# Two hybrid blocks on one Trainium2 core: dilated attention with bias and maximum in one instruction, queries scaled on GpSimd, block turns later, and spreads by transposes

## The reference

```python
def rms_norm_2(x, w):
    xf = x.astype(jnp.float32)
    y = xf * lax.rsqrt(jnp.mean(xf * xf, axis=-1, keepdims=True) + EPS)
    return (y * w.astype(jnp.float32)).astype(x.dtype)

# in second_block, for each layer:
q = rms_norm_2(q.reshape(b, s, ATT_HEADS, ATT_HEAD_DIM), q_norm[i])
k = rms_norm_2(k.reshape(b, s, ATT_HEADS, ATT_HEAD_DIM), k_norm[i])
y_att = dilated_attention(q, k, v).reshape(b, s, ATT_WIDTH)
x = x + jnp.concatenate([y_ssd, y_att], axis=-1) @ w_out[i]

# dilated_attention: for each of the branches ((128, 1), (512, 4), (2048, 16))
scores = jnp.einsum("bnqrhe,bnkrhe->bnrhqk", qb, kk).astype(jnp.float32)
scores = scores * (1.0 / math.sqrt(e))
scores = jnp.where(valid, scores, -jnp.inf)     # causal, one key in `dilation`
p = jnp.exp(scores - jnp.max(scores)); o = (p / den) @ v
# the three branches are then weighed by the softmax of their log denominators
```

## Time and profile before

| what | us |
|---|---|
| median of three runs | 1941.1 (1940.7 to 1943.38) |
| the profiled execution, its time | 1941.14 |
| its span, first to last instruction | 1939.3 |
| TensorE busy | 1912.3 (99%) |
| DVE, ACT, GpSimd busy | 1440.1, 1156.5, 375.9 |

### The profile page before, as it was taken

One profiled execution on the slowest core, in us unless ns is written; L12 is line 12 of the kernel. 1 busy time (PEld: TensorE's weight loads), 2 busy tenths in 40 slices (PEclk: granted clock), 3 DMA queues, 4 the chain that ended last, 5 costly groups with the idle time before them and its releaser, 6 DMA issues.

```text
span 1939.3 us, 30473 instructions
## 1 busy us (share of the span) xinstructions
PE 1912.3 (99%) x11704; PEld 1666.5 (86%) x11704; DVE 1440.1 (74%) x2535; ACT 1156.5 (60%) x2112; POOL 375.9 (19%) x424
## 2 busy tenths in 40 slices
PE   9999999999999999999999999999999999999999
PEld 8878998887899988888887788888888897878887
DVE  5866976576688759765687878866885678887874
ACT  6666765565676545554666655555554566656552
POOL 1110222011012104420012204411440002122430
PEclk9999999999999999999999999999999999999999
DMA  8434556543445555555553346555555544345654
GB/s 299 139 104 146 186 185 234 178 135 124 139 160 190 198 186 181 188 189 171 183 172 103 109 162 193 189 195 181 188 192 190 182 154 152 98 137 180 192 189 128
DMA packets 90687, 329.91 MB, mean 170 GB/s; under 512 B 10032, under 2 KB 10416, under 8 KB 90288
## 3 DMA queue, kind: packets, MB, share of 16 engines
q1 hardware_dynamic: 90544, 327.98, 51.5%
HBM read 326.89 MB, written 1.05 MB: 169 GB/s over the span
## 4 chain that ended last, share of the span: by engine, by line
PE 87%; DVE 7%; ACT 4%; issue 1%; DMA 1%; SPq 0%; DVEq 0%; ACTq 0%
PE PS L83 85%; PE PS L86 2%; DVE WL L98 2%; ACT TMP L95 1%; DVE TMP L108 1%; ACT WH L92 1%; DVE SM L114 1%; DMA RAW<-wts 1%; DVE SM L108 0%; ACT M L92 0%; ACT M L95 0%; SPq L80 0%; ACT TMP L92 0%; DVE SM L98 0%; DVE X L98 0%
## 5 line engine op out<-in xcount | busy, mean ns | idle before, releaser
L98 DVE TENSOR_TENSOR WL<-RAW,WH 128x1024 fp32r<-128x1024 f32 (+1 forms) x609 | 756.0, 1246 | 329.8 <-ACT WH L92 325.4
L92 ACT ACTIVATE WH<-RAW 128x1024 fp32r<-128x1024 f32 (+1 forms) x609 | 640.2, 1055 | 320.9 <-PE PS L83 314.1
L83 PE MATMUL PS<-WH,GX 128*128 128x512 f32 (+1 forms) x1632 | 524.7, 392 | 4.9 <-DVE GX L98 4.7
L83 PE MATMUL PS<-HX,WH 128*128 128x512 f32 (+1 forms) x1888 | 520.8, 345 | 3.4 <-DVE HX L108 1.5
L83 PE MATMUL PS<-GX,WH 128*128 128x256 f32 (+1 forms) x2208 | 461.7, 302 | 1.6 <-DVE WL L98 0.8
L83 PE MATMUL PS<-HX,WL 128*128 128x256 f32 x1472 | 413.2, 281 | 0.0
L83 PEld LDWEIGHTS PS<-GX,WH 128*128 128x128 f32 x2208 | 353.9, 189 | 21.0 <-issue 1.2
L83 PEld LDWEIGHTS PS<-HX,WH 128*128 128x128 f32 x1888 | 327.4, 189 | 50.3 <-DVE WL L98 2.9
L83 PEld LDWEIGHTS PS<-WH,GX 128*128 128x128 f32 x1632 | 305.6, 188 | 69.2 <-DVE WL L98 3.7
L83 PE MATMUL PS<-GX,WL 128*128 128x256 f32 x1280 | 361.5, 282 | 0.0
L83 PE MATMUL PS<-WL,GX 128*128 128x512 f32 (+1 forms) x816 | 316.6, 388 | 0.0
(11 more groups left out here) (139 smaller groups left out, 1668.3 us busy)
## 6 DMA issues: line engine op xcount, KB each, us to landing
RAW<-wts SPq DMA_DIRECT2D x607, 512.0 KB, 4.1
M<-bias SPq DMA_DIRECT2D x4, 512.0 KB, 11.2
M<-bias SPq DMA_DIRECT2D x1, 2048.0 KB, 9.8
X<-x SPq DMA_DIRECT2D x2, 512.0 KB, 5.6
TMP<-mem SPq DMA_DIRECT2D x1, 1024.0 KB, 12.0
out<-X SPq DMA_DIRECT2D x4, 256.0 KB, 3.4
CST<-cst SPq DMA_DIRECT2D x1, 714.0 KB, 9.7
RAW<-wts SPq DMA_DIRECT2D x2, 256.0 KB, 5.6
```

What stands on the lines that cost most here:

```text
L83: return Issued(self.eng and self.eng.matmul(o, l, r, start=first, stop=last, skip_group_check=share))
L92: return Issued(self.eng.activation(o, i, f, scale=scale))
L98: return Issued(self.eng and self.eng.tensor_tensor(o, a, b, op))
```

## The change

DVE's two `stt` and two `peak` of a head become two `least` (tensor_tensor_reduce): minus the sum of scores and bias, with its minimum as the accumulator output. The exponential is then taken with a scale of -1. The queries' factors can no longer be applied there, so GpSimd multiplies all four raw blocks, in the order 0, 1, 2, 3, each with four instructions. The turns of block 0 go from n == 5 and 6 to n == 13, of block 1 from n == 13 to n == 15, of block 3 from steps 3 and 4 of `("v2", L, 0)` to steps 4 and 6 of `("v2", L, 1)`, with banks 0 and 1 in place of 6 and 7 for blocks 0 and 3. ACT's `features` go along. Raw block 3 lies in `SQ`. `put_over` transposes the broadcast column.

```diff
--- before.py
+++ after.py
@@ -115,6 +115,9 @@
 
     def total(self, o, i):
         return Issued(self.eng and self.eng.tensor_reduce(o, i, AX.X, ALU.add))
+
+    def least(self, o, a, b, sign, acc):
+        return Issued(self.eng and self.eng.tensor_tensor_reduce(o, a, b, sign, 3e38, ALU.add, ALU.min, acc))
 
     def recip(self, o, i):
         return Issued(self.eng and self.eng.reciprocal(o, i))
@@ -291,7 +294,9 @@
 
         def raw_t(b, t):
 
-            o = (4096, 10240, 11264, 5120)[b] + t * 512
+            if b == 3:
+                return SQ.rearrange("p k s -> p (k s)")[:, t * 512:t * 512 + 512]
+            o = (4096, 10240, 11264)[b] + t * 512
             return M[:, o:o + 512]
 
         def sq_wide(t):
@@ -331,10 +336,6 @@
 
         PREP_RATES = [0, 0, 0] + [0, 1, 0] + [1, 1, 0] + [0, 0, 0] + [1, 0, 0] * 5
         DIL_PARTS = [0, 0, 0] + [2, 2, 1] + [1, 1, 0] * 2 + [0, 1, 0] * 5
-
-        def place(j):
-
-            return j if j < 4 else j + 8 if j < 8 else j - 4
 
         SSD_RATE = 1.5
 
@@ -443,12 +444,12 @@
                 p0, m = 64 * (h % 2), h // 2
                 hs.append(dict(q=[Q2[p0:p0 + 64, m, t * 128:t * 128 + 128] for t in range(2)],
                                k=[K2[p0:p0 + 64, m, 0:128], K2[p0:p0 + 64, m, :]],
-                               scale=[SCL[:, t, 2 * place(m) + h % 2:2 * place(m) + h % 2 + 1] for t in range(2)],
+                               scale=None,
                                bias=cc(C_LC, 384),
                                v=[V2[:, t, h * 64:h * 64 + 64] for t in range(2)], dst=m,
                                q_by=(aout, ("qkt", L, 0 if m < 4 else 3, m % 4 // 2)),
                                k_by=(aout, ("qkt", L, 1 + m // 4, m % 4 // 2)), v_by=("v2", L, h // 8),
-                               scale_by=("scl", L, m // 4)))
+                               scale_by=None))
             return hs
 
         def keys_of(widths, t):
@@ -612,7 +613,7 @@
 
                 ps = take(key, allowed)
                 for t in range(2):
-                    m = e.mm(ps[:, t * 128:t * 128 + 128], cols[t], ident, True, True)
+                    m = e.turn(ps[:, t * 128:t * 128 + 128], cols[t], ident)
                 m.then_inc(spread, key)
 
             def rms_over(st, allowed=WHOLE):
@@ -832,10 +833,7 @@
                 def turn_qk(b, q, allowed):
 
                     ps = take(("qkt", L, b, q), allowed)
-                    if b in (1, 2):
-                        e.wait_ge(scaled, ("k2", L, b, q))
-                    else:
-                        e.wait_ge(aout, ("qk", L, b))
+                    e.wait_ge(scaled, ("k2", L, b, q))
                     for i in range(4):
                         t, f = i % 2, 2 * q + i // 2
                         m = e.turn(ps[:, i * 128:i * 128 + 128], raw_t(b, t)[:, f * 128:f * 128 + 128], ident)
@@ -889,16 +887,17 @@
                         dt_raw()
                     if n == 3:
                         dt_turn()
-                    if n in (5, 6):
-                        turn_qk(0, n - 5, (6, 7))
                     if n == 9:
                         dt_sums()
-                    if n == 13:
+                    if n in (13, 15):
                         for q in range(2):
-                            turn_qk(1, q, (0, 1))
+                            turn_qk(n // 2 - 6, q, (0, 1))
 
                 def others():
-                    yield from tm_wide(("v2", L, 1), mix, 512, (2, 7))
+                    for i, _ in enumerate(tm_wide(("v2", L, 1), mix, 512, (2, 7))):
+                        if i in (4, 6):
+                            turn_qk(3, i // 2 - 2, (0, 1))
+                        yield
                     for m in range(8):
                         fm_tile(("z", L, m), whole, WT if m >= 2 else (0, 1))
                         yield
@@ -928,8 +927,6 @@
                 for i, _ in enumerate(tm_wide(("v2", L, 0), mix, 512, (0, 1))):
                     if i in (1, 2):
                         turn_qk(2, i - 1, (6, 7))
-                    if i in (3, 4):
-                        turn_qk(3, i - 3, (6, 7))
                     if i == 5:
                         next(dilated)
                 run(dilated)
@@ -1107,11 +1104,14 @@
                     nm, den = smc(520 + 4 * (j % 4), 2), smc(522 + 4 * (j % 4), 2)
                     if j >= 4:
                         e.wait_ge(turned, (a, j - 4))
-                    e.wait_ge(small, (a, "max", j))
+                    if a[0] == "dil":
+                        e.wait_ge(dout, (a, "s", j))
+                    else:
+                        e.wait_ge(small, (a, "max", j))
                     src = src_t(j) if biased else bank((a, "s", j))
                     for t in range(2):
                         sl = keys_of(widths, t)
-                        m = e.act(ACT.Exp, exp_t(a, j)[:, sl], src[:, sl], scale=1.0 if biased else h["scale"][t],
+                        m = e.act(ACT.Exp, exp_t(a, j)[:, sl], src[:, sl], scale=-1.0 if a[0] == "dil" else 1.0 if biased else h["scale"][t],
                                   bias=nm[:, t:t + 1], acc=den[:, t:t + 1])
                         if t == 0:
                             m.then_inc(exped, (a, j, 0))
@@ -1490,16 +1490,14 @@
                         e.wait_ge(small, ("ab", L))
                         e.act(ACT.Exp, U_, AB_, scale=-1.0).then_inc(ready, ("u", L))
                         e.act(ACT.Exp, EA, PAR[:, pb + Q_AL:pb + Q_AL + 16]).then_inc(ready, ("ea", L))
-                    if n in (6, 7):
-                        features(0, n - 6)
                     if n == 10:
                         e.wait_ge(ssd, ("cumt", L))
                         for o in (0, 32):
                             i = e.act(ACT.Copy, CUM[o:o + 16, :], bank(("cumt", L))[o:o + 16, 0:256])
                         i.then_inc(ready, ("cumt", L))
                     if n == 14:
-                        features(1, 0)
-                        features(1, 1)
+                        for q in range(2):
+                            features(0, q)
 
                 def z_tanh(m):
                     key = ("z", L, m)
@@ -1511,6 +1509,8 @@
                 def others():
                     for i in range(KD):
                         highs((("v2", L, 1), i))
+                        if i in (4, 6):
+                            features(3, i // 2 - 2)
                         yield
                     values_out(("v2", L, 1), V2, 512, ("rx", ("mix2", L)))
                     for m in range(8):
@@ -1529,8 +1529,11 @@
                         raw_out(3)
                     if i % 2 == 0 and i < 6:
                         behind(16 + i // 2)
-                    if 2 <= i < 6:
-                        features(2 + (i - 2) // 2, i % 2)
+                    if i == 1:
+                        for q in range(2):
+                            features(1, q)
+                    if 2 <= i < 4:
+                        features(2, i % 2)
                     if i == 6:
                         next(dilated)
                 values_out(("v2", L, 0), V2, 0, ("rx", ("mix2", L)))
@@ -1763,7 +1766,8 @@
                     h = heads[j]
                     nm = smc(520 + 4 * (j % 4), 2)
                     ab = bank((a, "s", j))
-                    e.wait_ge(small, h["scale_by"])
+                    if a[0] != "dil":
+                        e.wait_ge(small, h["scale_by"])
                     e.wait_ge(scored, (a, j))
                     if h["bias"] is not None:
                         src = src_t(j)
@@ -1771,6 +1775,12 @@
                             e.wait_ge(exped, (a, j - 2))
                         if a[0] == "na":
                             e.wait_ge(bias_in, a[1])
+                        if a[0] == "dil":
+                            for t in range(2):
+                                sl = keys_of(widths, t)
+                                m = e.least(src[:, sl], ab[:, sl], h["bias"][:, sl], -1.0, nm[:, t:t + 1])
+                            m.then_inc(dout, (a, "s", j))
+                            return
                         for t in range(2):
                             sl = keys_of(widths, t)
                             m = e.stt(src[:, sl], ab[:, sl], h["scale"][t], h["bias"][:, sl], ALU.mult, ALU.add)
@@ -1778,11 +1788,7 @@
                         e.wait_ge(dout)
                     else:
                         src = ab
-                    if widths[0] == widths[1]:
-                        e.peak(nm, src[:, 0:tot].rearrange("p (t k) -> p t k", t=2)).then_inc(small, (a, "max", j))
-                    else:
-                        for t in range(2):
-                            e.peak(nm[:, t:t + 1], src[:, keys_of(widths, t)]).then_inc(small, (a, "max", j))
+                    e.peak(nm, src[:, 0:tot].rearrange("p (t k) -> p t k", t=2)).then_inc(small, (a, "max", j))
                     if h["bias"] is None:
                         e.wait_ge(small)
```

(4 more changed lines are left out.)

## The result

| | before | after |
|---|---|---|
| median of 7 runs each, us | 1943.38 (1940.7 to 1945.47) | 1948.12 (1945.55 to 1949.31) |
| the profiled execution, us | 1941.14 | 1949.15 |
| its span, us | 1939.3 | 1947.3 |

The changed kernel is slower by a quarter of a per cent: ratio 1.0027, 95% interval 1.0018 to 1.0037. Most executions of the kernel before lie near one of four steps about 2.1 us apart (1939.0, 1941.2, 1943.4, 1945.5), and its profiled one is in a low step. So the ledger further down compares spans, and the forecast of +2.8, which started from 1941.1, is held against the +8.0 of the spans there, not against the +4.7 of the medians.

A forecast was written before the change was run, and what follows sets the result against it. TensorE, busy 1912.3 of 1939.3 us, was taken as the bound. Two layers of a 4.36 us wait less 1.5 recovered, minus 2.9 for spreads, gave +2.8 on 1941.1: 1943.9 us, range 1937.5 to 1949.5.

The forecast's parts named there:

- the fall of the clock: Rival: TensorE's rest before v2,0 halves its pace there, 1.7 us a fall; 1947.3 us with one per layer; chance 0.25.
- The wait before v2,0: Block 1's turn at n == 15 makes TensorE wait for ACT to empty banks 0 and 1: 4.36 us a layer.
- The wait before xd2: Block 3's moved turns reorder banks 0 and 1; xd2 waits about 1.5 us for DVE, replacing 0.80: 0.55 a layer more.
- The fused instruction: Bias and maximum in one DVE instruction: 0.82 us a head, saving 1.39 a pair, 22 us of DVE time.
- Recovered in the pairs: Dilated stage: shorter DVE work removes TensorE waits of 1.10 and 0.51 us and some later: 1.5 us a layer net.
- GpSimd: Scaling block 3's queries takes 3.75 us, leaving 1.3 before head 0's division; rival, it becomes late: 1946.5 us, chance 0.11.
- The spreads: Sixteen put_over calls by transposes, all on TensorE's path, 0.18 us less each: 2.9 us less in all.

The follow-up runs named there:

- x1: Changed kernel, but ACT runs block 1's two features before raw_out(3), so banks 0 and 1 are freed sooner: 1939.09 us, ratio 0.9981 to the kernel before.
- x2: Changed kernel with the turns of blocks 0 and 1 spread half by half over n == 12 to 14: 1936.49 us, ratio 0.9969 to the kernel before.
- x7: x2 with block 3's second turn one step later (i == 7, not 6), on TensorE and ACT: 1933.73 us, ratio 0.9957 to the kernel before.
- x6: x7 without the fused instruction, a separate addition and maximum in its place: 1934.21 us, ratio 0.9965 to the kernel before.
- x4: Kernel before with one edit, put_over by transposes: 1939.17 us, ratio 0.9980 to the kernel before.
- x7_again: x7 unchanged, run and profiled once more: 1933.79 us.
- x5: Changed kernel with 10 dummy f32 matmuls before v2,0, so TensorE works through the wait: 1944.3 us, ratio 1.0015 to the kernel before.
- x3: Changed kernel with 21 dummy f32 matmuls before v2,0, which outlasted the wait: 1953.42 us, ratio 1.0052 to the kernel before.
- a_again: The changed kernel unchanged, repeated on another chip (also called the repeat): 1948.97 us, ratio 1.0048 to the kernel before.
- b_again: The kernel before, unchanged, profiled a second time: 1940.88 us.

## Why the prediction was right, and where it was wrong

1943.9 us was forecast and 1948.12 measured; the range held it, and that is in part luck. Of the 4.2 us between the two, 2.3 are the starting point (1941.1, where the seven runs of the kernel before have 1943.38) and 1.9 the change (+2.8 against +4.7). In spans the forecast was +2.8 and the trace shows +8.0, and in the repeat the medians are 9.9 apart. The main mechanism was right; a second one that hangs on it, the fall of the clock, stood among the rivals and not in the sum.

**The wait before v2,0: right.** Forecast 4.36 us a layer, measured 4.40 from start to start, with a row of 4.25. The code gave the place and ACT's own rows the size. x1 and x2 show that it can be removed and what it costs.

**The clock: the step that failed.** The forecast took the wait at its own length and gave the fall a chance of 0.25, with "the clock column full throughout" as the argument against. That argument carried no weight: the longest of the waits there was 1.10 us, so a full column said nothing of 4.25 us. The one case of rest that the trace did have, the start of the kernel, showed half pace, and pointed the other way. It should have been the likelier case. The section "What's actually happening" of "TensorE: Matmul & The Clock Gate" in the Trainium skill, by which an idle array returns to the lower clock, agrees with what the runs show here: half pace behind 4.25 us of rest, full pace behind 1.53 us, and behind 4.48 us of dummy matmuls. Its price was taken as 1.7 us a fall from the earlier trace rows; the first layer gave 1.65, the second 2.93: there the slow pace began with the first matmul and lasted until 1628.3, 6.0 us, where in the first layer it lasted from 1014.43 at the latest to about 1018. The rival's own figure, 1947.3, is 1.9 us under the profiled execution's 1949.15.

**The wait before xd2: right.** Forecast about 1.5 us, measured 1.36 and 1.37. x7 shows that it is the order on banks 0 and 1: one step later, it is gone.

**The fused instruction: the saving right, its parts not.** DVE's timeline of the kernel after, one pair:

```profile
1040.99 0.28 DVE L120 CUSTOM_DVE_ANT_0 TMP<-PS,CST 128x128 f32<-128x128 f32 x1
1041.20 0.09 DVE L120 DVE_READ_ACCUMULATOR2_ANT SM<- 128x1 f32 x1
1041.20 0.42 DVE L120 CUSTOM_DVE_ANT_0 TMP<-PS,CST 128x256 f32<-128x256 f32 x1
1041.55 0.09 DVE L120 DVE_READ_ACCUMULATOR2_ANT SM<- 128x1 f32 x1
1041.55 0.29 DVE L120 CUSTOM_DVE_ANT_0 TMP<-PS,CST 128x128 f32<-128x128 f32 x1
```

I had taken 0.82 us a head, the means of the `stt` rows, as the fused instruction should be no shorter. It is: its means are 286 and 419 ns, 0.71 us a head, and the start-to-start distance is 0.21 + 0.35 = 0.56 us. The old rows overlapped too: a pair took 2.59 us from 1043.98 to 1046.57 in the kernel before, not 2 x 1.51. With the fused instruction it takes 1.20, from the first start to the end of the last read. So a pair saves 2.59 - 1.20 = 1.39 us, which is the forecast's number, by two errors that cancel. DVE's busy time fell by 19.5 us where 22 were forecast. The Trainium skill's "Two Vector instructions with no wait between them" in "VectorE: DVE Perf Modes" is borne out as to the count, two records each. The smaller saving that the forecast drew from it isn't there: the read of the accumulator takes 0.09 us and starts together with the next instruction.

**Recovered in the pairs: the size nearly right, its cause only in part.** Forecast 1.5 us a layer, measured 1.75. The wait of 1.10 us is gone (1.16 by the starts, where 1.26 was put), so is that of 0.51 (0.62); xd2 takes 0.68 back where 0.55 was forecast; the last pairs gave 0.67 where 0.3 was put. The forecast put all of this down to the shorter instruction. x6 shows that without it most of the first wait is gone already (0.38 is left), and that the fused instruction adds 1.1 us a layer to the 1.96 that x6 has.

**GpSimd: right, closer than I put it.** Its rows of the kernel after:

```profile
991.33 10.77 POOL L98 TENSOR_TENSOR M<-M,SM 128x256 f32<-128x256 f32 x12 [139.54 <-DVE SM L104]
1026.06 4.22 POOL L98 TENSOR_TENSOR SQ<-SQ,SM 128x256 f32<-128x256 f32 x4 [23.96 <-DVE SM L105]
1030.53 1.70 POOL L105 TENSOR_SCALAR TMP<-TMP,SM 128x128 f32<-128x128 f32 x4 [0.26 <-DVE SM L123]
```

Block 3 took 4.22 us, not 3.75, and GpSimd then waited 0.26 us for DVE before the first division. It is not late, but of the margin of 1.3 us one fifth is left.

**The spreads: mis-sized.** Forecast 2.9 us, measured 2.0 in x4. 0.16 to 0.18 us each holds for the first four, which have matmuls right behind them. Of the later ones a part goes into waits that open behind them: in x4 TensorE waits 0.23 us for DVE behind the last two of the first layer and 0.18 behind those of the second (0.25 and 0.17 in x7_again), where the kernel before doesn't wait. 32 records on the transposing line stand where 64 were, as forecast:

```profile
L86 PE MATMUL PS<-CST,SM x32: 270/272/323, 27.3 to 1772.6; 128*128 128x128 f32 x32
```

In all: forecast 2 x (4.36 - 1.5) - 2.9 = 2.8; measured 2 x (4.40 - 1.75) - 2.0 = 3.3, and 4.6 for the clock.

## What to carry to other kernels

Before you move an instruction onto a PSUM bank that is wanted again at once, count what stands on the reading engine ahead of its copy: here a weight copy, four squares and copies, a band and a silu made a rest of 4.25 us out of a move that costs TensorE nothing. A rest of TensorE of this length is to be priced at its length plus what the slow clock takes behind it (1.65 and 2.93 us here), and a clock row that is full in a kernel without such rests is no evidence against that. And look at what stands behind a gain or a loss: a slow stretch ahead of two waits cost 0.2 us, the same clock ahead of a dense stretch cost up to 2.9.

## What the runs showed of the hardware that was not expected

- The granted clock fell (0.66 to 0.69 over 5 us where one window holds the whole fall) behind sixteen matmul records of one column with no rest before them. Each layer of the second block has two such stretches, and it fell behind the first of a layer alone: in both layers of the kernel after and of x5, in one in x1, x3, x4, x7_both, x7_again, a_again and b_again, in none in the first profile of the kernel before, in x2 and in x6. That these records bring it down is not shown.
- The f32 matmul of 128x256 on plain f32 operands leaves two records and takes 0.42 us, twice what I had reckoned from one record; the transposes of 128x128 leave one each.
- `CUSTOM_DVE_ANT_0`, the fused instruction, is shorter than the scalar_tensor_tensor of the same shape: 286 against 343 ns for 128 columns and 419 against 475 for 256, and its accumulator is read in 82 ns beside the next one.
- Executions of one kernel lie in steps of 2.1 us, at a granted clock of 0.999 or 1.000 in the kernel before. One such step is a pace of TensorE that is 2% lower in the first SwiGLU of the second block (110.5 against 108.4 us), without a wait and at a granted clock of 1.00. Its cause was not found.
